# Values, index key and token scalars of a hybrid attention block as one token-major product, 340 columns wide

## The chip, the cores and the metric

The kernel runs on one core of a Trainium2 chip. The metric is the time of one execution on the device in microseconds (us); the median of three runs before the change is 1101.5 us. The engines are TensorE (PE in the profile, with its weight loads as PEld), VectorE (DVE), ScalarE (ACT), GpSimd (POOL) and SyncE (SP). Each works through its own list of instructions in order and waits on semaphores for the others.

## What is computed

Two layers of a block on 256 tokens with 1024 features: a mixer (sparse attention and a gated delta rule from one input projection), cross attention to a memory, and a gated feed-forward. The change touches the start of the mixer alone. Cut to that:

```
h = rms_norm(x) * gain
proj = h @ w_in
a_q, a_k, a_v, i_q, i_k, i_w, b_qkv, b_a, b_b, g_a, g_b = split(proj)
q, k, qi, ki = rope(a_q), rope(a_k), rope(i_q), rope(i_k)      # ki: 64 columns, the index key
g    = -exp(a_log) * softplus(b_a + dt_bias)                    # 8 columns per token
beta = sigmoid(b_b)                                             # 8 columns per token
score = sum over 4 index heads of i_w * relu(qi . ki)           # i_w: 4 columns per token
sel = the 64 best keys of each token, by score
y_a = softmax attention of q over the selected k and v          # v: 256 columns
y_b = gated_delta_rule(conv(b_qkv), g, beta)
```

## The kernel before, in words

Activations lie feature-major: `h` has features on partitions and tokens in columns. A weight is read in **slabs** of 128 x 1024 floats (512 KB), 322 in all, in the order of the list `ORDER` that `stream_of` makes. SyncE fetches each slab into one of five places (`RAWS`), ScalarE rounds it into one of four places (`HIGHS`; function `highs`, L381), GpSimd (a few times VectorE) makes the rest that the rounding lost (function `lows`, L391), and TensorE then multiplies three times: high by high, low by high, high by low (function `product`, L494 to L496). So every logical product is three matmuls. A slab's fetch waits until the slab five before it has been used, its rounding until the one four before it has.

Most products are **feature-major**: the weight block is the stationary operand, 256 tokens stream past, and the result has features on partitions. They take one slab each, 8 blocks of 128 features, 24 matmuls 256 columns wide (`wide_half`). The values are **token-major**: a 128 x 128 piece of `h` is the stationary operand and the weight's columns stream past.

At the start of the mixer TensorE's list is: index queries `iq` (2 slabs), `small` (1 slab: feature-major, 20 token scalars and the 64 index-key columns padded to 128 rows), keys `k` (2 slabs), the transposes of the 20 scalar rows (L613), values `v` (2 slabs, token-major), queries `q0` (2 slabs), the index `logits` (L636, which wait for the rotated index query and key), `q1` to `q3` (2 slabs each), and the `decay` products (L670). Then come `bk0`, `bk1` and so on. PSUM banks are handed out in turn by `claim`, which waits for the last reader of a bank: `bk1` takes the bank of `q2`, and so waits for its rotation.

VectorE's list there: rotation of `iq` (L1879 to L1884), of the index key (L1894 to L1899), of `k`; then the **gate chain** (L1912 to L1926: sixteen columns, thirteen small steps that go to ScalarE and back for an exponential and a logarithm); four products `g_upto` (L1930), `beta` (L1932), the rotation of `q0`, and the score of token tile 0 (L1950 to L1953), followed by its top-64 search.

ScalarE's list decides when slabs are rounded. `copy` first calls `high_parts`, which rounds slabs up to a fixed count, and then waits for what it copies. One place matters: the relus of the second token tile wait for the first tile's score, because they overwrite its input, and no slab behind the second one of `q2` is rounded ahead of them:

```
                    if c == 1:

                        act.wait_ge(*dve_idx.at(layer, ("score", 0)))
```

## Time and profile before

| | |
|---|---|
| median of three runs (lowest, highest) | 1101.5 us (1101.43, 1101.6) |
| profiled execution, first to last instruction (span) | 1099.9 us |
| around the span, median less span | 1.6 us |
| mean granted TensorE clock | 0.999 of full speed |
| TensorE / VectorE / ScalarE / GpSimd busy | 99% / 51% / 51% / 61% |
| HBM read | 179.47 MB |

The profiled execution's own time outside its span is not recorded apart; the difference to the median stands for it. How to read it: matmuls are pipelined, so the busy share of TensorE says that something is always in flight, not that it works at its peak. The distance from one start to the next tells what a matmul costs.

### The profile page before, as it was taken

The page shows a single profiled execution, that of the slowest core. Times are in us where ns is not written, and L with a number is a line of the kernel's source. Part 1 is how long each engine was busy: PE and PEld are TensorE (multiplying, and loading weights), DVE is VectorE, ACT ScalarE, POOL GpSimd, SP SyncE. Part 2 cuts the span into 40 slices and gives each one's busy share as a digit, 9 for nine tenths or more (in the row PEclk, how much of TensorE's full clock was granted, in tenths as well). Part 3 has the DMA queues.
Part 4 walks back from the last instruction along what each step waited for, and adds up shares of the span by engine and source line. Part 5 has one row for each costly group of instructions (what it writes and reads, how often), then busy time and mean ns, then how long its engine had stood idle before and what let it go on. Part 6 is the DMA issues. An engine that isn't in the chain of part 4 may idle for free.

```text
span 1099.9 us, 19903 instructions
## 1 busy us (share of the span) xinstructions
PE 1089.6 (99%) x8135; PEld 1014.0 (92%) x8138; DVE 559.5 (51%) x1082; ACT 561.2 (51%) x888; POOL 670.2 (61%) x351
## 2 busy tenths in 40 slices
PE   8999999999999999999999999999999999999997
PEld 7999999998898999999999999999989979999996
DVE  6788479354515631223358866793644344212234
ACT  7645864435655544444464567544356554444442
POOL 4876769627673457654377758685378454586442
PEclk9999999999999999999999999999999999999999
DMA  7443544624543655555555444445155255555553
GB/s 291 173 154 135 188 130 163 180 74 170 194 153 125 205 188 186 180 189 180 184 173 173 157 141 164 152 156 163 69 194 194 97 181 178 191 179 187 187 180 112
DMA packets 63337, 183.37 MB, mean 167 GB/s; under 512 B 18576, under 2 KB 19088, under 8 KB 63248
## 3 DMA queue, kind: packets, MB, share of 16 engines
q1 hardware_dynamic: 47936, 172.48, 45.3%
q10 hardware_dynamic: 15312, 9.64, 3.4%
q8 instruction: 64, 1.05, 0.4%
q14 instruction: 25, 0.20, 0.1%
HBM read 179.47 MB, written 2.62 MB: 166 GB/s over the span
## 4 chain that ended last, share of the span: by engine, by line
PE 97%; ACT 1%; DVE 1%; DMA 1%; POOL 0%; issue 0%; SPq 0%; DVEq 0%; ACTq 0%; POOLq 0%
PE psum L494 28%; PE psum L495 27%; PE psum L496 27%; PE psum L658 1%; PE psum L985 1%; PE psum L964 1%; PE psum L699 1%; PE psum L1086 1%; PE psum L588 1%; PE psum L879 1%; PE psum L872 1%; PE psum L754 1%; DMA sb_raw<-weights 1%; PE psum L682 1%; PE psum L843 0%; PE psum L670 0%
## 5 line engine op out<-in xcount | busy, mean ns | idle before, releaser
L391 POOL TENSOR_TENSOR sb_low<-sb_raw,sb_high 128x1024 fp32r<-128x1024 f32 x257 | 616.5, 2413 | 337.3 <-ACT sb_high L381 323.1
L381 ACT ACTIVATE sb_high<-sb_raw 128x1024 fp32r<-128x1024 f32 x322 | 340.1, 1061 | 406.4 <-DMA sb_raw<-weights 361.6
L494 PE MATMUL psum<-sb_h_high,sb_high 128*128 128x256 f32 x1640 | 463.9, 283 | 0.0
L495 PE MATMUL psum<-sb_h_low,sb_high 128*128 128x256 f32 x1640 | 463.3, 282 | 0.0
L496 PE MATMUL psum<-sb_h_high,sb_low 128*128 128x256 f32 x1640 | 462.5, 282 | 0.0
L494 PEld LDWEIGHTS psum<-sb_h_high,sb_high 128*128 128x128 f32 x1640 | 310.3, 189 | 1.8 <-DVE sb_region_c L1879 0.3
L496 PEld LDWEIGHTS psum<-sb_h_high,sb_low 128*128 128x128 f32 x1640 | 308.6, 188 | 0.0
L495 PEld LDWEIGHTS psum<-sb_h_low,sb_high 128*128 128x128 f32 x1640 | 307.7, 188 | 0.9
L391 DVE TENSOR_TENSOR sb_low<-sb_raw,sb_high 128x1024 fp32r<-128x1024 f32 x65 | 85.4, 1314 | 95.4 <-ACT sb_high L381 95.0
L1992 DVE SCALAR_TENSOR_TENSOR sb_conv<-psum,sb_param,sb_conv 128x255 f32<-128x255 f32 (+1 forms) x144 | 58.2, 473 | 37.0 <-ACT sb_conv L1405 36.8
L2248 DVE SCALAR_TENSOR_TENSOR sb_sq<-sb_th,psum 128x512 f32<-128x512 f32 x22 | 15.1, 687 | 110.0 <-ACT sb_th L1610 110.0
L495 PE MATMUL psum<-sb_low,sb_ff 128*128 128x512 f32 x176 | 69.7, 396 | 0.0
L496 PE MATMUL psum<-sb_high,sb_ff 128*128 128x512 f32 x176 | 69.7, 396 | 0.0
L494 PE MATMUL psum<-sb_high,sb_ff 128*128 128x512 f32 x176 | 69.7, 396 | 0.0
L496 PEld LDWEIGHTS psum<-sb_high,sb_ff 128*128 128x128 f32 x176 | 33.1, 188 | 8.0
L495 PEld LDWEIGHTS psum<-sb_low,sb_ff 128*128 128x128 f32 x176 | 33.2, 188 | 7.2
L494 PEld LDWEIGHTS psum<-sb_high,sb_ff 128*128 128x128 f32 x176 | 33.1, 188 | 7.2
L494 PE MATMUL psum<-sb_mem_high,sb_high 128*128 128x256 f32 x128 | 38.2, 298 | 1.0 <-DVE sb_mem_low L1734 1.0
L2252 DVE SCALAR_TENSOR_TENSOR psum<-sb_sq,psum 128x512 f32<-128x512 f32 x21 | 14.6, 696 | 48.1 <-PE psum L496 48.1
L496 PE MATMUL psum<-sb_mem_high,sb_low 128*128 128x256 f32 x128 | 36.1, 282 | 0.0
L495 PE MATMUL psum<-sb_mem_low,sb_high 128*128 128x256 f32 x128 | 36.0, 282 | 0.0
L2207 DVE TENSOR_REDUCE sb_tiny<-psum 128x2 f32<-128x512 f32 x8 | 5.6, 694 | 50.4 <-PE psum L964 50.4
(307 smaller groups left out, 1549.0 us busy)
## 6 DMA issues: line engine op xcount, KB each, us to landing
sb_raw<-weights SPq DMA_DIRECT2D x322, 512.0 KB, 3.2
sb_pre_gain<-pre_gains ACTq DMA_DIRECT2D x6, 512.0 KB, 4.4
sb_post_gain<-post_gains ACTq DMA_DIRECT2D x6, 512.0 KB, 4.5
sb_kx<-mem SPq DMA_DIRECT2D x2, 512.0 KB, 4.4
sb_x<-x SPq DMA_DIRECT2D x1, 1024.0 KB, 10.7
t_dram<-sb_sq ACTq DMA_DIRECT2D x4, 256.0 KB, 2.9
out<-sb_x SPq DMA_DIRECT2D x4, 256.0 KB, 2.0
m_dram<-sb_m ACTq DMA_DIRECT2D x8, 64.0 KB, 2.1
```

The lines of the kernel that those rows point to most:

```text
L381: nc.scalar.activation(high[:, n % HIGHS, :], raw[:, n % RAWS, :], ACT.Copy).then_inc(high_ready, 1)
L391: eng.tensor_tensor(low[:, k, :], raw[:, k, :], high[:, n % HIGHS, :].bitcast(F32), ALU.subtract).then_inc(low_ready[k], 1)
L494: pe.matmul(out, a[0], b[0], start=start, stop=False, **kw)
L495: pe.matmul(out, a[0], b[1], start=False, stop=False, **kw)
L496: return pe.matmul(out, a[1], b[0], start=False, stop=stop, **kw)
L588: tr = pe.transpose(o[:, k * P:(k + 1) * P], xn[:, c, b * P:(b + 1) * P], ident)
L658: mm = pe.matmul(o[:, i * P:(i + 1) * P], conv[:, hd, c * P:(c + 1) * P], conv[:, other + hd, c * P:(c + 1) * P], start=True, stop=True)
L682: mm = pe.matmul(misc[:, 16 * c + 2 * j + b:16 * c + 2 * j + b + 1], sq[:, j % 2, b * S + c * P:b * S + (c + 1) * P], one, start=True, sto ...
L699: pe.matmul(o[:, i * keys:(i + 1) * keys], q[:, hd, c * P:(c + 1) * P], kT[:, hd // (HEADS // KV_HEADS), 0:keys], start=True, stop=False, ...
L1992: V.scalar_tensor_tensor(out=conv[:, blk, d:S], in0=bank(CONV_SLOTS[j])[:, b * S:(b + 1) * S - d], scalar=tap(3 - d, blk), in1=conv[:, blk ...
L2248: link(V.scalar_tensor_tensor(out=sq[:, i % 2, :], in0=th[:, i % 2, :], scalar=1.0, in1=bank(("gate", i)), op0=ALU.add, op1=ALU.mult), dve ...
L2252: V.scalar_tensor_tensor(out=ff_tok if turned else bank(("up", i)), in0=sq[:, i % 2, :], scalar=0.5, in1=bank(("up", i)), op0=ALU.mult, op ...
```

## The change

The values, the index key and the token scalars become one weight of 256 + 64 + 20 = 340 columns (`BY_TOKEN`), laid into three slabs of 3, 3 and 2 feature blocks (`KS_OF`). TensorE multiplies it token-major: two token tiles, each in a bank of its own (5 and 6), eight feature blocks, three matmuls, that is 48 matmuls 340 columns wide in the place of the 24 of `small` and the 48 of `v`, all 256 wide. The number of slabs stays 322. The scalars come out token-major and aren't transposed any more; the index key is, after `k`. VectorE now does the gate chain ahead of the rotations of `k` and of the index key. ScalarE copies the index key, the scalars and, behind the logarithm, the values.

```diff
@@ -50,6 +50,9 @@
 HALF = KT * P
 FF_SLOTS = FF // 256
 TOKENWISE = IDX_HEADS + 2 * G_HEADS
+KV_COLS = KV_HEADS * DH
+BY_TOKEN = KV_COLS + IDX_DIM + TOKENWISE
+KS_OF = tuple(range(3 * b, min(3 * b + 3, KT)) for b in range(3))
 both = lambda part, *which: [(part, i, b) for i in which for b in range(2)]
 
 
@@ -57,7 +60,7 @@
     first, more = layer == 0, layer + 1 < DEPTH
     return (
         (both("xk", 0, 1) + [("xk", 2, 0)] if first else both("xk", 1, 2))
-        + both("iq", 0) + [("small", 0, 0)] + both("k", 0) + both("v", 0) + both("q", *range(4))
+        + both("iq", 0) + [("vs", 0, b) for b in range(3)] + both("k", 0) + both("q", *range(4))
         + both("bk", *range(4)) + both("bq", *range(4)) + both("bv", *range(4)) + both("ga", *range(4)) + both("gb", *range(4))
         + ([("xk", 2, 1)] if first else []) + both("xk", 3) + both("xv", 0) + [("xv", 1, 0)]
         + both("out", *range(4))
@@ -230,7 +233,7 @@
         idx_val = ra_t[:, 1024:1536].rearrange("p (c s) -> p c s", c=TILES)
         iq = rb_t[:, 0:512].rearrange("p (b t) -> p b t", b=2)
         ik = rb_t[:, 512:768]
-        small_feat = rb_t[0:TOKENWISE, 768:1024]
+        ik_tok = rb_t[:, 768:768 + 2 * IDX_DIM].rearrange("p (c n) -> p c n", c=TILES)
         rope_tmp = rc_t[:, 0:1024].rearrange("p (b n) -> p b n", b=2)
         p1 = ra_t[:, :].rearrange("p (h s) -> p h s", h=HEADS)
         t_up = grp(ra_t)
@@ -604,24 +607,20 @@
                 pe.wait_ge(*dve_part.at(layer, ("h_low", "mix", 1, 0)))
 
                 wide(("iq", 0), h, (dve_rope, "iq"), (4,), waits={4: dve_part.at(layer, ("h_low", "mix", 1, 1))})
-                o = claim(("small", 0), (dve_rope, "ik"), (5,))
-                wide_half(o[:, 0:S], HALF_AT[layer, "small", 0, 0], h).then_inc(slots.sem, mark(slots, ("small", 0)))
+                by_token = [claim(("vs", c), (act_copy, "v"), (5 + c,)) for c in range(TILES)]
+                for b in range(3):
+                    w = weights_here(HALF_AT[layer, "vs", 0, b])
+                    for c in range(TILES):
+                        for k in KS_OF[b]:
+                            at = slice((k - KS_OF[b][0]) * BY_TOKEN, (k - KS_OF[b][0] + 1) * BY_TOKEN)
+                            mm = product(by_token[c][:, 0:BY_TOKEN], pick(h, lambda t: t[:, k, c * P:(c + 1) * P]), pick(w, lambda t: t[:, at]), k == 0, k == KT - 1)
+                    mm.then_inc(slots.sem, mark(slots, ("vs", 0) if b == 2 else ("vs", 0, b)))
                 wide(("k", 0), h, (dve_rope, "k"))
-                o = claim("small_tok", (dve_gate, "x"), (3,), False)
-                pe.wait_ge(*act_copy.at(layer, "small"))
+                o = claim("ik_turned", (dve_rope, "ik"), (3,), False)
+                pe.wait_ge(*act_copy.at(layer, "ik"))
                 for c in range(TILES):
-                    tr = pe.transpose(o[:, c * TOKENWISE:(c + 1) * TOKENWISE], small_feat[:, c * P:(c + 1) * P], ident[0:TOKENWISE, 0:TOKENWISE])
-                tr.then_inc(pe_t.sem, mark(pe_t, "small_tok"))
-                o = claim(("v", 0), (act_copy, "v"))
-                for b in range(2):
-                    w = weights_here(HALF_AT[layer, "v", 0, b])
-                    for c in range(TILES):
-                        for k4 in range(4):
-                            k = 4 * b + k4
-                            mm = product(o[:, c * 256:(c + 1) * 256], pick(h, lambda t: t[:, k, c * P:(c + 1) * P]),
-                                         pick(w, lambda t: t[:, k4 * 256:(k4 + 1) * 256]), k == 0 and c == 0, k == KT - 1 and c == 1,
-                                         skip_group_check=True)
-                    mm.then_inc(slots.sem, mark(slots, ("v", 0) if b else ("v", "first")))
+                    tr = pe.transpose(o[0:IDX_DIM, c * P:(c + 1) * P], ik_tok[:, c, :], ident)
+                tr.then_inc(pe_t.sem, mark(pe_t, "ik_turned"))
                 wide(("q", 0), h, (dve_rope, ("q", 0)))
 
                 pe.wait_ge(*dve_rope.at(layer, "iq"))
@@ -1360,11 +1359,10 @@
                     act.wait_ge(masks_loaded, 32)
                     nc.scalar.activation(after_t[:, :], after, ACT.Copy).then_inc(after_ready, 1)
 
-                high_parts(ahead(("small", 0), 3))
-
-                copy(small_feat, bank(("small", 0))[0:TOKENWISE, 0:S], slots, ("small", 0), act_copy, "small")
-                copy(small, bank("small_tok")[:, 0:2 * TOKENWISE].rearrange("p (c n) -> p c n", c=TILES), pe_t, "small_tok", act_copy, "small_tok")
-                act.wait_ge(*act_copy.at(layer, "small_tok"))
+                by_token = psum[:, 5:7, :]
+                copy(ik_tok, by_token[:, :, KV_COLS:KV_COLS + IDX_DIM], slots, ("vs", 0), act_copy, "ik")
+                nc.scalar.activation(small, by_token[:, :, KV_COLS + IDX_DIM:BY_TOKEN], ACT.Copy).then_inc(act_copy.sem, act_copy.mark("small"))
+                act.wait_ge(*act_copy.at(layer, "small"))
                 nc.scalar.activation(beta, small[:, :, 12:20], ACT.Tanh, scale=0.5).then_inc(act_gdn.sem, act_gdn.mark("beta"))
                 nc.scalar.activation(a_exp, param_t[:, R_ALOG:R_ALOG + 8], ACT.Exp).then_inc(act_gdn.sem, act_gdn.mark("a"))
                 act.wait_ge(*dve_gate.at(layer, "abs"))
@@ -1372,7 +1370,7 @@
                 act.wait_ge(*dve_gate.at(layer, "w"))
                 nc.scalar.activation(ga_ln, ga_w, ACT.Ln).then_inc(act_gdn.sem, act_gdn.mark("ln"))
 
-                copy(flat(v_tok), bank(("v", 0)), slots, ("v", 0), act_copy, "v", scale=0.5)
+                nc.scalar.activation(v_tok, by_token[:, :, 0:KV_COLS], ACT.Copy, scale=0.5).then_inc(act_copy.sem, act_copy.mark("v"))
 
                 for c in range(TILES):
                     keys = (c + 1) * P
@@ -1885,16 +1883,16 @@
 
                 def rotate_ik():
 
-                    src = bank(("small", 0))[64:P, 0:S]
-                    tmp = rope_tmp[64:P, 1, 0:S]
-                    low_parts(ahead(("small", 0), 2))
-                    dve.wait_ge(*act_copy.at(layer, "small"))
-                    for lo in (64, 96):
+                    src = bank("ik_turned")[0:IDX_DIM, 0:S]
+                    tmp = rope_tmp[0:IDX_DIM, 1, 0:S]
+                    low_parts(ahead("ik_turned", 2))
+                    dve.wait_ge(*pe_t.at(layer, "ik_turned"))
+                    for lo in (0, 32):
                         o = lo ^ 32
-                        V.tensor_tensor(rope_tmp[lo:lo + 32, 1, 0:S], bank(("small", 0))[o:o + 32, 0:S], rope[o:o + 32, 3, :], ALU.mult)\
+                        V.tensor_tensor(rope_tmp[lo:lo + 32, 1, 0:S], src[o:o + 32], rope[o:o + 32, 3, :], ALU.mult)\
                             .then_inc(dve_rope.sem, dve_rope.mark(("partner", "ik", lo)))
-                    dve.wait_ge(*dve_rope.at(layer, ("partner", "ik", 96)))
-                    link(V.tensor_tensor(src, src, rope[64:P, 2, :], ALU.mult), dve_rope, ("cos", "ik"))
+                    dve.wait_ge(*dve_rope.at(layer, ("partner", "ik", 32)))
+                    link(V.tensor_tensor(src, src, rope[0:IDX_DIM, 2, :], ALU.mult), dve_rope, ("cos", "ik"))
                     V.tensor_tensor(ik[64:P], src, tmp, ALU.add).then_inc(dve_rope.sem, dve_rope.mark("ik_upper"))
                     link(V.tensor_tensor(ik[0:64], src, tmp, ALU.add), dve_rope, "ik")
 
@@ -1904,12 +1902,10 @@
                     dve.wait_ge(masks_loaded, 32)
                     dve.wait_ge(tables_act, 1)
                 rotate("iq", ("iq", 0), iq, 2, 2, 32, "iq", 0)
-                rotate_ik()
-                rotate("k", ("k", 0), kT, 2, 0, 64, "k", 0)
 
                 link(V.tensor_copy(upto_psum, upto), dve_gate, "upto")
-                dve.wait_ge(*act_copy.at(layer, "small_tok"))
-                link(V.tensor_tensor(ga_x, bank("small_tok")[:, 0:2 * TOKENWISE].rearrange("p (c n) -> p c n", c=TILES)[:, :, 4:12], heads(param_t[:, R_DT:R_DT + 8], TILES), ALU.add), dve_gate, "x")
+                dve.wait_ge(*act_copy.at(layer, "small"))
+                link(V.tensor_tensor(ga_x, small[:, :, 4:12], heads(param_t[:, R_DT:R_DT + 8], TILES), ALU.add), dve_gate, "x")
                 link(V.tensor_scalar(ga_abs, ga_x, -1.0, None, ALU.mult), dve_gate, "minus")
                 link(V.tensor_tensor(ga_abs, ga_x, ga_abs, ALU.max), dve_gate, "abs")
                 dve.wait_ge(*act_gdn.at(layer, "e"))
@@ -1924,6 +1920,8 @@
                 V.tensor_copy(g_tok, ga_x).then_inc(dve_gate.sem, dve_gate.mark("g"))
                 link(V.tensor_copy(g_round, ga_x), dve_gate, "g_round")
                 link(V.tensor_tensor(g_rest, ga_x, g_round.bitcast(F32), ALU.subtract), dve_gate, "g_rest")
+                rotate("k", ("k", 0), kT, 2, 0, 64, "k", 0)
+                rotate_ik()
                 for c in range(TILES):
 
                     for part, g_part in enumerate((g_round.bitcast(F32), g_rest)):
@@ -2318,11 +2316,9 @@
                 continue
             name = "xk" if name == "nk" else name
             to = stream[n]
-            if name == "small":
-                piece = blocks(np.concatenate([tokenwise, np.zeros((D, 64 - TOKENWISE), np.float32), part("ik")], 1))
-                to.reshape(P, KT, P)[:, :, 0:piece.shape[2]] = piece
-            elif name == "v":
-                to[:] = blocks(part("v")[512 * b:512 * (b + 1)]).reshape(P, HALF)
+            if name == "vs":
+                piece = blocks(np.concatenate([part("v"), part("ik"), tokenwise], 1))[:, list(KS_OF[b])]
+                to[:, 0:len(KS_OF[b]) * BY_TOKEN] = piece.reshape(P, -1)
             elif name in ("gate", "up") and i == 0 and layer + 1 == DEPTH:
                 to[:] = blocks(mats[name][512 * b:512 * (b + 1), 0:256]).reshape(P, HALF)
             elif name == "down":
```

VectorE at the start of the mixer in layer 0, before: from the end of the `iq` rotation (out `sb_region_b`) to the first step of the gate chain (`128x16`).

```order
L1884 TENSOR_TENSOR sb_region_b<-psum,sb_region_c 128x512
L1894 TENSOR_TENSOR sb_region_c<-psum,sb_rope_tables 32x256 x2
L1897 TENSOR_TENSOR psum<-psum,sb_rope_tables 64x256
L1898 TENSOR_TENSOR sb_region_b<-psum,sb_region_c 64x256
L1899 TENSOR_TENSOR sb_region_b<-psum,sb_region_c 64x256
L1879 TENSOR_TENSOR sb_region_c<-psum,sb_rope_tables 64x512 x2
L1883 TENSOR_TENSOR psum<-psum,sb_rope_tables 128x512
L1884 TENSOR_TENSOR sb_k_rope<-psum,sb_region_c 128x512
L1910 COPY psum<-sb_const 128x128
L1912 TENSOR_TENSOR psum<-psum,sb_param 128x16
```

The same engine and place now, from the `iq` rotation on:

```order
L1882 TENSOR_TENSOR sb_region_b<-psum,sb_region_c 128x512
L1906 COPY psum<-sb_const 128x128
L1908 TENSOR_TENSOR psum<-sb_tiny,sb_param 128x16
L1909 TENSOR_SCALAR sb_tiny<-psum 128x16
L1910 TENSOR_TENSOR sb_tiny<-psum,sb_tiny 128x16
```

And the end of the gate chain now, up to the first `g_upto` product (out `sb_g_high`):

```order
L1922 TENSOR_TENSOR sb_tiny<-psum,sb_g_round 128x16
L1877 TENSOR_TENSOR sb_region_c<-psum,sb_rope_tables 64x512 x2
L1881 TENSOR_TENSOR psum<-psum,sb_rope_tables 128x512
L1882 TENSOR_TENSOR sb_k_rope<-psum,sb_region_c 128x512
L1892 TENSOR_TENSOR sb_region_c<-psum,sb_rope_tables 32x256 x2
L1895 TENSOR_TENSOR psum<-psum,sb_rope_tables 64x256
L1896 TENSOR_TENSOR sb_region_b<-psum,sb_region_c 64x256
L1897 TENSOR_TENSOR sb_region_b<-psum,sb_region_c 64x256
L1928 TENSOR_TENSOR sb_g_high<-psum,sb_g_round 128x1024
```

Both rotations moved from ahead of the gate chain to behind it, the index key's last; the instructions are the same in number and size.

ScalarE in layer 0, before: roundings (L381), the copy of the feature-major scalars (`20x256`), the copy of the transposed ones (`128x40`), the gate chain's functions, roundings, values.

```order
L381 ACTIVATE sb_high<-sb_raw 128x1024 x3
L1327 ACTIVATE sb_region_b<-psum 20x256
L381 ACTIVATE sb_high<-sb_raw 128x1024 x2
L1327 ACTIVATE sb_tiny<-psum 128x40
L1368 ACT_TABLE_LOAD
L1368 ACTIVATE sb_tiny<-sb_tiny 128x16
L1369 ACTIVATE sb_tiny<-sb_param 128x8
L1371 ACTIVATE psum<-sb_tiny 128x16
L1373 ACT_TABLE_LOAD
L1373 ACTIVATE sb_tiny<-sb_tiny 128x16
L381 ACTIVATE sb_high<-sb_raw 128x1024 x2
L1327 ACTIVATE sb_v<-psum 128x512
```

The same place now, with the index key copied as `128x128`:

```order
L384 ACTIVATE sb_high<-sb_raw 128x1024 x5
L1326 ACTIVATE sb_region_b<-psum 128x128
L1364 ACTIVATE sb_tiny<-psum 128x40
L1366 ACT_TABLE_LOAD
L1366 ACTIVATE sb_tiny<-sb_tiny 128x16
L1367 ACTIVATE sb_tiny<-sb_param 128x8
L1369 ACTIVATE psum<-sb_tiny 128x16
L1371 ACT_TABLE_LOAD
L1371 ACTIVATE sb_tiny<-sb_tiny 128x16
L1373 ACTIVATE sb_v<-psum 128x512
```

All five roundings now stand ahead of the first copy, and the values are copied ahead of the next two roundings.

## Rows read from the trace of the kernel before

**Rows 1.** The page's line of busy us, shares of the span and counts.

```profile
PE 1089.6 (99%) x8135; PEld 1014.0 (92%) x8138; DVE 559.5 (51%) x1082; ACT 561.2 (51%) x888; POOL 670.2 (61%) x351
```

**Rows 2.** The waits of TensorE: who for whom, us in total, times, longest.

```profile
PE psum L452 <- DVE sb_th L1723: 1.5, 1, 1.5
```

**Rows 3.** Timeline of TensorE, layer 0: start us, us, engine, line, operation, out<-in.

```profile
33.38 0.28 PE L494 MATMUL psum<-sb_h_high,sb_high 128*128 128x256 f32 x1
...
53.99 1.68 PE L636 MATMUL psum<-sb_region_b 64*128 64x128 f32 x16
...
73.03 0.58 PE L670 MATMUL psum<-sb_g_high,sb_after 128*128 128x512 f32 x1
...
250.98 0.39 PE L494 MATMUL psum<-sb_high,sb_mem_high 128*128 128x512 f32 x1
...
253.54 0.40 PE L496 MATMUL psum<-sb_high,sb_mem_low 128*128 128x512 f32 x1
```

**Rows 4.** Timeline of VectorE, layer 0; in brackets the idle time before and who ended it.

```profile
38.27 0.88 DVE L1894 TENSOR_TENSOR sb_region_c<-psum,sb_rope_tables 32x256 f32<-32x256 f32 x2 [0.28 <-ACT sb_region_b L1327]
...
40.12 0.43 DVE L1899 TENSOR_TENSOR sb_region_b<-psum,sb_region_c 64x256 f32<-64x256 f32 x1
42.29 1.41 DVE L1879 TENSOR_TENSOR sb_region_c<-psum,sb_rope_tables 64x512 f32<-64x512 f32 x2 [1.75 <-PE psum L496]
...
45.20 0.30 DVE L1910 COPY psum<-sb_const 128x128 f32<-128x128 f32 x1
...
49.12 1.22 DVE L1930 TENSOR_TENSOR sb_g_high<-psum,sb_g_round 128x1024 fp32r<-128x1024 f32 x1
...
53.66 2.38 DVE L1932 TENSOR_SCALAR sb_tiny<-sb_tiny 128x16 f32<-128x16 f32 x1
...
59.16 0.35 DVE L1950 TENSOR_SCALAR psum<-sb_region_a,sb_tiny 128x128 f32<-128x128 f32 x1
```

**Rows 5.** Timeline of ScalarE, layer 0.

```profile
42.60 1.06 ACT L381 ACTIVATE sb_high<-sb_raw 128x1024 fp32r<-128x1024 f32 x1 [1.37 <-DMA sb_raw<-weights]
43.56 0.18 ACT L1327 ACTIVATE sb_tiny<-psum 128x40 f32<-128x40 f32 x1
...
46.16 0.19 ACT L1371 ACTIVATE psum<-sb_tiny 128x16 f32<-128x16 f32 x1 [0.79 <-DVE sb_tiny L1914]
```

**Rows 6.** Timeline of GpSimd, layer 0.

```profile
41.30 4.84 POOL L391 TENSOR_TENSOR sb_low<-sb_raw,sb_high 128x1024 fp32r<-128x1024 f32 x2 [0.19 <-ACT sb_high L381]
...
48.91 9.44 POOL L391 TENSOR_TENSOR sb_low<-sb_raw,sb_high 128x1024 fp32r<-128x1024 f32 x4 [2.76 <-ACT sb_high L381]
63.15 14.18 POOL L391 TENSOR_TENSOR sb_low<-sb_raw,sb_high 128x1024 fp32r<-128x1024 f32 x6 [4.80 <-ACT sb_high L381]
```

**Rows 7.** VectorE's L1734 in its two forms, and GpSimd beside it.

```profile
10.54 3.23 DVE L1734 SCALAR_TENSOR_TENSOR sb_mem_low<-psum,sb_param,sb_mem_high 128x256 fp32r<-128x256 f32 x8 [0.34 <-ACT sb_mem_high L1202]
...
342.95 5.68 DVE L1734 SCALAR_TENSOR_TENSOR sb_mem_low<-sb_mem_feat,sb_param,sb_mem_high 128x256 fp32r<-128x256 f32 x4 [1.45 <-ACT sb_mem_high L1193]
...
10.29 2.38 POOL L391 TENSOR_TENSOR sb_low<-sb_raw,sb_high 128x1024 fp32r<-128x1024 f32 x1 [2.00 <-DVE sb_low L391]
...
345.87 2.47 POOL L391 TENSOR_TENSOR sb_low<-sb_raw,sb_high 128x1024 fp32r<-128x1024 f32 x1 [0.86 <-ACT sb_high L381]
```

**Rows 8.** Layer 1: timelines of ScalarE, VectorE, GpSimd and TensorE.

```profile
585.62 1.06 ACT L381 ACTIVATE sb_high<-sb_raw 128x1024 fp32r<-128x1024 f32 x1 [1.81 <-DMA sb_raw<-weights]
...
589.20 0.19 ACT L1371 ACTIVATE psum<-sb_tiny 128x16 f32<-128x16 f32 x1 [2.08 <-DVE sb_tiny L1914]
...
596.69 0.16 DVE L1932 TENSOR_SCALAR sb_tiny<-sb_tiny 128x16 f32<-128x16 f32 x1
...
586.76 2.40 POOL L391 TENSOR_TENSOR sb_low<-sb_raw,sb_high 128x1024 fp32r<-128x1024 f32 x1 [0.49 <-ACT sb_high L381]
...
604.04 7.27 POOL L391 TENSOR_TENSOR sb_low<-sb_raw,sb_high 128x1024 fp32r<-128x1024 f32 x3 [2.48 <-ACT sb_high L381]
...
616.06 0.58 PE L670 MATMUL psum<-sb_g_high,sb_after 128*128 128x512 f32 x1
```

## The prediction, written before the changed kernel ran

> **What bounds the kernel now.** I read the page first: TensorE is busy 99% of the span, everyone else at most 61% [rows 1]. A busy share alone can mislead for pipelined matmuls, so the list of waits came second: TensorE's longest wait is 1.5 us, at the very start [rows 2], and none lies in the stretch that the change touches, in either layer. So TensorE's own stream is the bound there, and taking columns off it pays, as long as no wait appears that had been covered. Third came TensorE's timeline, for what a matmul costs: the distance between starts, not the 0.28 us shown. From the first matmul of `small` at 33.38 to the logits at 53.99 are 20.61 us; seven slabs are 168 matmuls, 256 wide, and the two scalar transposes with their changes of kind take the rest; 168 x 0.120 = 20.16. At 512 columns eleven steps from 250.98 to 253.54 give 0.233 us [rows 3]. Last, the timelines of VectorE, ScalarE and GpSimd in the same stretch, to see how much cover their chains have: that is where this case is decided.
>
> **TensorE's part.** Per layer 24 + 48 matmuls of 256 columns go (72 x 0.120 = 8.64 us) and 48 of 340 come. No row has 340 columns. The bounds are 0.120 (as 256 wide) and 0.233 (as 512 wide) [rows 3]; cost grows with width, so I take the straight line between them, 0.120 + 84/256 x 0.113 = 0.157 us, nearer the 256 end. 48 x 0.157 = 7.54 us, a saving of 1.1 us per layer, 2.2 in all. The two transposes stay two, moved behind `k`; I cost the move at nothing. The slabs, their bytes and the rounding work are the same in number, and a slab is used in 18, 18 and 12 matmuls instead of 24, which asks for the next ones sooner.
>
> The Trainium skill ("TensorE: Matmul & The Clock Gate", Back-to-back issue gap) gives N/2.4 GHz + 2.5 ns. By that rule, as an estimate, 340 columns cost 0.144 us and the saving is 1.7 us per layer; the trace differs from it, 0.120 against its 0.109 at 256 columns. By it the sum below would be about 1 us lower.
>
> **VectorE's chain, layer 0.** Before, the index key is rotated from 38.27 to 40.55 and `k` from 42.29 to 45.20 [rows 4], while the scalars are still on their way. Now both rotations (2.3 + 2.9 = 5.2 us) stand behind the gate chain, and the logits wait for the index key. So the question is when the gate chain can start and end.
>
> Its input comes through ScalarE, which now rounds five slabs before it copies. The last of them (the second of `q0`) is fetched when the second new slab has been used, at 33.38 + 36 x 0.157 = 39.04. Before, the fetch waited for the slab that ended at 39.15 and the rounding started at 42.60 [rows 5]; now 42.5. Before, the scalars' copy followed at 43.56; now one more short copy stands between (estimate 0.3, from the 0.18 of the small one): the scalars are ready at about 43.95.
>
> The first gate step changes its operands. It was `psum<-psum,sb_param`; now it is `psum<-sb_tiny,sb_param`, with both inputs in SBUF. What that means is in two rows of one line, L1734: with one input in PSUM eight instructions take 3.23 us while GpSimd's 2.38 us operation runs beside them; with both in SBUF four take 5.68 us instead of 1.6, and the last ends at 348.63, 0.28 after GpSimd's operation from 345.87 to 348.34 [rows 7]. An instruction with both inputs in SBUF does not get through beside a GpSimd operation; it waits for its end. `beta` (L1932), all in SBUF, shows the same: 2.38 us from 53.66, where GpSimd's operations run, and 0.16 at 596.69, in a gap between two [rows 4, 6, 8]. The Trainium skill says so too ("SBUF — State Buffer", Who interferes with whom): two SBUF inputs contend with a GpSimd instruction that reads SBUF, and the one that comes second is blocked until the first has finished.
>
> GpSimd works on the two `q0` slabs from 41.30 to 46.14 [rows 6], now 0.1 us earlier at most. The first gate step therefore starts at 43.95 and ends at 46.15, not at 44.15. Its bounds are 0.18 (no conflict) and 2.4 (a whole operation). From there to the exponential (46.16 before) it is 0.45 us: 46.6, that is 0.4 later than before. The rest of the chain takes as long as before, to 49.12 + 0.4; then come the rotations, 5.2 us: the index key is ready at 54.8. Before, the logits started at 53.99. So TensorE, which could have been there at 52.9, starts them 0.8 us late: the saving is gone in that wait.
>
> Everything behind is shifted more: `g_upto` starts at 54.8 instead of 49.12, 5.65 later. `beta` gives some of it back: GpSimd's four operations, from 48.91 to 58.35 before, run some 0.9 later now (0.4 for the chain, 0.5 for the values' copy put ahead of the roundings) and end at about 59.3, just when `beta` comes; nothing follows them until the score is done. `beta` costs 0.2 instead of 2.38. The score of tile 0 then starts 3.5 us later than at 59.16.
>
> That score releases the relus of tile 1, and behind them the rounding of the first `q3` slab, whose rest GpSimd makes from 63.15 on, after 4.80 us of idling [rows 6]. TensorE reaches that slab 48 matmuls before 73.03, at 67.2 [rows 3]: a cover of 67.2 - 65.5 = 1.7 us. Now the rest is ready at 63.15 + 3.5 + 2.4 = 69.05, and TensorE, 0.8 late, arrives at 68.0. It goes on at 69.1: **+1.9 us in layer 0**. Queued behind the waiting relus are all of ScalarE's roundings, so this is the wait that counts; from the next slab on GpSimd (2.4 us) is faster than TensorE (2.88 us) again.
>
> **Layer 1.** The rounding that was at 585.62 is at 585.5 [rows 8], the scalars are ready at 587.0, and GpSimd is in the operation that began at 586.76 (now 586.65, to 589.05). The first gate step ends at 589.1, the exponential is at 589.55, 0.35 later. The logits start 0.7 late by the same count. `beta` was short before, so nothing is given back: the score is 0.35 + 5.2 = 5.6 us later. GpSimd's operation of 604.04 moves to 609.65 and ends at 612.05. TensorE was there at 616.06 - 5.8 = 610.25, now at 610.95; it goes on at 612.1: **+1.85 us**.
>
> **Sum.** +1.9 + 1.85 = +3.8 us on a span of 1099.9: 1103.7. The median is 1.6 above that span, so the forecast is 1105.3 us. No term is owed for the 2.2 us of saved columns: in both layers the end is set by VectorE's chain. Only the columns of the first two new slabs count, since they set when the last rounding is released: the chain moves with 36 of them. Priced as 256 wide (36 x 0.037 = 1.3 us earlier in each layer) the sum is +1.2, 1102.7; priced as 512 wide (36 x 0.076 = 2.7 later) it is +9.2, 1110.7.
>
> **Rivals.**
>
> *No conflict at the first gate step.* For: it is 16 columns wide and might slip in between GpSimd's accesses, and no row shows so small an operation with two tensors in SBUF. Against: L1932 is as small and did wait. Then the exponential waits for ScalarE's table load alone: 0.6 earlier than before in layer 0 (it had idled 0.79, the scalars come 0.2 later), 1.55 earlier in layer 1 (it had idled 2.08). Layer 0: logits 0.25 early, `beta` held until the four operations end, score 2.4 later, slab ready at 67.95: +0.75. Layer 1: logits 1.1 early, score 3.8 later, slab at 610.2: 0. Together +0.8: 1102.3 us.
>
> *The saved columns come through.* The chain is covered everywhere and 2.2 us go: 1099.3 us. For it speaks that TensorE waits nowhere now. Against: the covers are 1.7 us at the `q3` slab in layer 0 and about 3.8 in layer 1, and 5.2 us of rotations are put in front of what has them. It needs the gate chain to end some 3 us sooner than before.
>
> *`beta` held as well: clearly slower.* In both layers `beta` comes within 0.1 us of the end of GpSimd's run. If it comes just after the last operation has begun, because a rounding was late, it is held for up to 2.4 us, and the score, the `q3` slab and TensorE with it. The point is whether the last of the four operations ends before VectorE has done `g_upto`. In one layer that makes +2.1: 1107.4 us.
>
> *340 columns cost like 512*: 1110.7 us, as above.
>
> **How the numbers follow.** The forecast 0.62, no conflict 0.17, `beta` held 0.10, dear columns 0.05, saving comes through 0.06. A measurement of this kernel can tell about 0.2% from no change, 2.2 us. Slower by more than that (over 1103.7) are nearly all of the forecast's outcomes (0.57), `beta` held and dear columns: 0.72. Within it are the case without conflict, a few of the forecast's, and half of the last: 0.24. Faster: 0.04. The range reaches from the case without conflict with some room, 1101.8, to the one with `beta` held, 1107.5; outside are the saving that comes through, dear columns and little else.
>
> **What the changed profile would show.** Matmuls with 340 columns start 0.157 us apart. L1908 of the changed kernel (the first gate step) takes about 2.2 us in both layers and ends with a GpSimd operation; at 0.18 us the first rival is right. The gate chain then starts 0.4 us later than before, and `beta` (L1930 there) is short in layer 0. TensorE has waits that it had not: for `dve_rope` ahead of the logits, 1.9 us in layer 0 and 1.8 in layer 1, and for the rest of the first `q3` slab, 1.1 us in each. If the second of these is missing, the forecast is wrong, wherever the time comes out.

## The result, and the profile after

The changed kernel takes 1106.32 us (median of four runs, 1106.18 to 1107.84), the kernel before 1101.51: a ratio of 1.0044, 95% interval 1.0032 to 1.0057. So the change made it 0.4% slower. A repetition (e11 below) gave 1.0049 (1.0036 to 1.0062). The forecast was 1105.3 us, slower. The profiled execution has a span of 1104.5 us, 4.6 more than before. What follows first shows where these 4.6 us are, and then, by twelve runs, what causes them.

First the list of TensorE's waits in the changed kernel (who waits for whom: us in total, times, longest). Against [rows 2] two are new, the first and the last shown: the index logits (L635) wait for VectorE's rotation of the index key, and a product (L497) waits for GpSimd to finish the rest of a slab. Both stand in the stretch that the change touches.

```profile
PE psum L635 <- DVE sb_region_b L1897: 4.4, 2, 2.5
PE psum L455 <- DVE sb_th L1721: 1.5, 1, 1.5
PE psum L497 <- DVE sb_mem_low L1732: 1.0, 1, 1.0
PE psum L461 <- DVE sb_kx L1727: 1.0, 2, 0.7
PE psum L497 <- POOL sb_low L394: 0.9, 1, 0.9
```

Then TensorE's timeline (start us, us, engine, line, operation; in brackets the idle time before and who ended it), which answers to [rows 3]. From the first 340 wide matmul to the last are 47 steps, 7.33 us: 0.156 us each, where 0.157 was forecast.

```profile
33.75 0.32 PE L497 MATMUL psum<-sb_high,sb_h_high 128*128 128x340 f32 x1
...
41.08 0.32 PE L499 MATMUL psum<-sb_high,sb_h_low 128*128 128x340 f32 x1
...
55.60 1.68 PE L635 MATMUL psum<-sb_region_b 64*128 64x128 f32 x16 [2.48 <-DVE sb_region_b L1897]
...
76.08 0.58 PE L669 MATMUL psum<-sb_g_high,sb_after 128*128 128x512 f32 x1
...
600.38 1.65 PE L635 MATMUL psum<-sb_region_b 64*128 64x128 f32 x16 [1.91 <-DVE sb_region_b L1897]
...
614.66 0.36 PE L497 MATMUL psum<-sb_h_high,sb_high 128*128 128x256 f32 x1 [0.92 <-POOL sb_low L394]
```

Layer 1 shows both waits, as forecast. Layer 0 has no wait for a slab, and the prediction said of that wait that without it the forecast is wrong, wherever the time comes out. And yet from the logits (55.60) to the decay products (76.08) it needs 20.48 us where before it needed 19.04. The busy time by stretch says why (from:to, length, PE busy us and count, granted clock, DMA share, GB/s):

```profile
53.00:56.00 3.00, 0.52 (x8) 1.00 0.53 183
56.00:57.00 1.00, 1.00 (x14) 1.00 0.00 0
57.00:58.00 1.00, 1.00 (x6) 0.55 0.00 0
58.00:60.00 2.00, 2.00 (x12) 0.50 0.00 0
60.00:61.00 1.00, 1.00 (x8) 0.74 0.00 0
61.00:62.00 1.00, 1.00 (x10) 1.00 0.00 0
```

Behind the idle stretch (53.1 to 55.6) the granted clock is 0.50, 1.2 GHz, for some 3 us; the 256 wide matmuls there start 0.213 us apart and not 0.120. That makes this part 1.45 us longer. The Trainium skill describes it ("TensorE: Matmul & The Clock Gate", What's actually happening): a monitor halves the clock of a TensorE that has been idle. The trace agrees, and e5 and e10 below put it to the test.

VectorE's timeline answers to [rows 4], ScalarE's to [rows 5], GpSimd's to [rows 6]:

```profile
44.83 2.15 DVE L1908 TENSOR_TENSOR psum<-sb_tiny,sb_param 128x16 f32<-128x16 f32 x1 [6.14 <-ACT sb_tiny L1364]
...
50.38 1.41 DVE L1877 TENSOR_TENSOR sb_region_c<-psum,sb_rope_tables 64x512 f32<-64x512 f32 x2
...
55.54 1.23 DVE L1928 TENSOR_TENSOR sb_g_high<-psum,sb_g_round 128x1024 fp32r<-128x1024 f32 x1
...
60.07 0.17 DVE L1930 TENSOR_SCALAR sb_tiny<-sb_tiny 128x16 f32<-128x16 f32 x1
...
63.36 0.35 DVE L1948 TENSOR_SCALAR psum<-sb_region_a,sb_tiny 128x128 f32<-128x128 f32 x1
```

```profile
43.40 1.06 ACT L384 ACTIVATE sb_high<-sb_raw 128x1024 fp32r<-128x1024 f32 x1 [2.36 <-DMA sb_raw<-weights]
44.37 0.26 ACT L1326 ACTIVATE sb_region_b<-psum 128x128 f32<-128x128 f32 x1
44.52 0.20 ACT L1364 ACTIVATE sb_tiny<-psum 128x40 f32<-128x40 f32 x1
...
47.43 0.19 ACT L1369 ACTIVATE psum<-sb_tiny 128x16 f32<-128x16 f32 x1 [1.08 <-DVE sb_tiny L1910]
```

```profile
44.54 2.40 POOL L394 TENSOR_TENSOR sb_low<-sb_raw,sb_high 128x1024 fp32r<-128x1024 f32 x1 [0.91 <-ACT sb_high L384]
50.66 9.36 POOL L394 TENSOR_TENSOR sb_low<-sb_raw,sb_high 128x1024 fp32r<-128x1024 f32 x4 [3.72 <-ACT sb_high L384]
67.36 4.75 POOL L394 TENSOR_TENSOR sb_low<-sb_raw,sb_high 128x1024 fp32r<-128x1024 f32 x2 [7.35 <-ACT sb_high L384]
```

These rows show three things. VectorE idles 6.14 us ahead of the first gate step, where it used to rotate. That step (L1908) takes 2.15 us and ends within 0.05 us of GpSimd's operation beside it (44.54 + 2.40). And from the gate chain (44.83) to the score (63.36) VectorE has one unbroken row of work, 18.5 us long, in which it waits for another engine only twice, for ScalarE's two functions, 0.96 us together. The row simply starts too late.

**Where the 4.6 us are.** I measure one stretch of TensorE's list in each layer, from the first index-query matmul to the first of `bk0` (27.90 to 79.17 in layer 0 after the change). Before it is 48.49 us in each layer; after, 51.27 and 50.28. Layer 0: -1.31 (from the first matmul of the product to the point where the logits could start are 19.30 us, not 20.61), +2.55 of standing still ahead of the logits, +1.45 of low clock, +0.09 in the index query: +2.78. Layer 1: -1.31, +1.98 ahead of the logits, +1.12 for the slab: +1.79. Together 4.57 of the 4.6.

### The profile page after: what moved, and what is told of

The parts are those of the page before. It is cut to its first block, busy times and chain, and to the rows that moved or that the text cites. A ratio compares the mean times of both kernels' runs of the same rounds, so it can differ in the third digit from the quotient of the medians.

```text
span 1104.5 us, 19808 instructions
## 1 busy us (share of the span) xinstructions
PE 1088.7 (99%) x8090; PEld 1013.1 (92%) x8090; DVE 565.2 (51%) x1082; ACT 559.9 (51%) x888; POOL 672.1 (61%) x351
## 4 chain that ended last, share of the span: by engine, by line
PE 93%; DVE 3%; DMA 1%; ACT 1%; issue 1%; POOL 0%; SPq 0%; DVEq 0%; ACTq 0%; POOLq 0%
PE psum L497 26%; PE psum L498 26%; PE psum L499 26%; PE psum L657 1%; PE psum L984 1%; DMA sb_raw<-weights 1%; PE psum L963 1%; PE psum L698 1%; PE psum L1085 1%; PE psum L591 1%; PE psum L878 1%; PE psum L871 1%; PE psum L753 1%; PE psum L681 1%; ACT sb_high L384 1%
## 5 line engine op out<-in xcount | busy, mean ns | idle before, releaser
L497 PE MATMUL psum<-sb_h_high,sb_high 128*128 128x256 f32 x1624 | 461.4, 284 | 0.9 <-POOL sb_low L394 0.9
L498 PE MATMUL psum<-sb_h_low,sb_high 128*128 128x256 f32 x1624 | 458.5, 282 | 0.0
L497 PEld LDWEIGHTS psum<-sb_h_high,sb_high 128*128 128x128 f32 x1624 | 307.1, 189 | 3.3 <-issue 1.8
L497 PE MATMUL psum<-sb_high,sb_ff 128*128 128x512 f32 x176 | 69.7, 396 | 0.0
L497 PEld LDWEIGHTS psum<-sb_high,sb_ff 128*128 128x128 f32 x176 | 33.1, 188 | 7.2
L497 PE MATMUL psum<-sb_mem_high,sb_high 128*128 128x256 f32 x128 | 38.2, 298 | 1.0 <-DVE sb_mem_low L1732 1.0
```

Source lines behind the costliest of these rows:

```text
L497: pe.matmul(out, a[0], b[0], start=start, stop=False, **kw)
L498: pe.matmul(out, a[0], b[1], start=False, stop=False, **kw)
```

## The experiments

For each kernel its two stretches in us, in one profiled execution (before: 48.49 and 48.49), and its median beside that of the kernel before, run next to it on the same chip. The ratio is worked out from all runs, so it can differ a little from that of the two medians:

| kernel | layer 0 | layer 1 | median | before | ratio, 95% |
|---|---|---|---|---|---|
| changed | 51.27 | 50.28 | 1106.32 | 1101.51 | 1.0044 (1.0032 to 1.0057) |
| e1 gate step from PSUM | 49.90 | 48.33 | 1103.88 | 1102.30 | 1.0016 (1.0007 to 1.0024) |
| e2 index key first | 53.75 | 51.80 | 1109.71 | 1102.30 | 1.0064 (1.0051 to 1.0077) |
| e3 score first | 52.86 | 52.52 | 1110.70 | 1102.30 | 1.0082 (1.0059 to 1.0106) |
| e4 both | 53.81 | 53.28 | 1115.66 | 1102.30 | 1.0119 (1.0106 to 1.0132) |
| e5 long filler | 52.20 | 51.74 | 1109.77 | 1102.64 | 1.0063 (1.0049 to 1.0077) |
| e6 before, new order | 49.25 | 49.00 | 1104.33 | 1102.64 | 1.0016 (1.0007 to 1.0025) |
| e7 changed, old order | 54.24 | 53.08 | 1112.88 | 1102.64 | 1.0093 (1.0079 to 1.0107) |
| e8 copy sooner | 51.22 | 49.63 | 1107.89 | 1102.64 | 1.0048 (1.0034 to 1.0062) |
| e9 as e8, and beta later | 47.88 | 47.75 | 1101.49 | 1101.91 | 0.9994 (0.9985 to 1.0002) |
| e10 short filler | 51.39 | 50.34 | 1107.05 | 1101.91 | 1.0048 (1.0034 to 1.0062) |
| e11 changed again | 51.57 | 50.69 | 1107.60 | 1101.91 | 1.0049 (1.0036 to 1.0062) |
| e12 as e9, and score 1 sooner | 48.26 | 47.48 | 1101.59 | 1102.05 | 0.9995 (0.9986 to 1.0004) |

**e1: is it the two SBUF inputs?**

```diff
-link(V.tensor_tensor(ga_x, small[:, :, 4:12], ...), dve_gate, "x")
+link(V.tensor_tensor(ga_x, psum[:, 5:7, KV_COLS + IDX_DIM + 4:KV_COLS + IDX_DIM + 12], ...), dve_gate, "x")
```

> The changed kernel with one operand changed: the first gate step reads the scalars from the product's PSUM banks and not from ScalarE's copy in SBUF; it still waits for that copy, so its place and its wait are the same. Theory (two SBUF inputs are blocked by the GpSimd operation beside them): the step takes 0.18 us and not 2.15. In layer 0 ScalarE is busy until 46.35, so the exponential comes only 1.0 us sooner; in layer 1 2.0 sooner. Logits wait 1.4 us in layer 0, too short for the clock to fall, and none in layer 1; the wait for the first q3 slab's rest is about 0.9 in each. Sum about -3.5: 1102.8 us. Rival (the step waits for something else, such as ScalarE's copy or a semaphore): it still takes about 2.15 us and the time stays at 1106.3.

The step's row on VectorE, and GpSimd's beside it:

```profile
44.71 0.18 DVE L1908 TENSOR_TENSOR psum<-psum,sb_param 128x16 f32<-128x16 f32 x1 [6.35 <-ACT sb_tiny L1364]
```

```profile
44.43 2.39 POOL L394 TENSOR_TENSOR sb_low<-sb_raw,sb_high 128x1024 fp32r<-128x1024 f32 x1 [0.91 <-ACT sb_high L384]
```

Same place, same wait, same neighbour: 0.18 us instead of 2.15, in layer 1 as well. The cause of that term is shown: it is the second input from SBUF beside a GpSimd operation. The time falls to 1.0016 of the kernel before, 1.58 us over it where 1.3 was expected; waits of 1.5 us (index key, layer 0) and 0.9 (slab, in each layer) are left, and the clock stays at 1.00.

**e2, e3, e4: are TensorE's waits in series?** e2 swaps two calls. e3 moves six instructions, the four `g_upto` products, `beta` and its neighbour, behind the score of tile 0. e4 does both.

```diff
-rotate("k", ("k", 0), kT, 2, 0, 64, "k", 0)
 rotate_ik()
+rotate("k", ("k", 0), kT, 2, 0, 64, "k", 0)
```

> The changed kernel with one edit: VectorE rotates the index key ahead of k. The logits can then start when TensorE arrives (index key ready at 52.6 in layer 0, TensorE there at 53.1), but k, g_upto, beta, the rotation of q0 and the score come at the same time as now. Theory (both waits hang on one chain, in series): nothing is won, TensorE idles about 3.4 us in layer 0 and 2.8 in layer 1 for the rest of the first q3 slab instead, and if the clock falls after such a wait it costs up to 1.4 us in each: 1105.9 to 1108.7, I expect 1107.3. Rival (waits add up, each can be taken away alone): the 4.4 us of waiting for the index key and 1.4 of low clock go: 1100.5.

The wait of the logits goes, and waits of 3.77 and 2.92 us for the slab come, each with the low clock (some 25 and 15 slow matmuls). TensorE's timeline, then its stretches; in layer 0 the clock fell at 69.3, while TensorE was still waiting:

```profile
70.50 0.55 PE L497 MATMUL psum<-sb_h_high,sb_high 128*128 128x256 f32 x1 [3.77 <-POOL sb_low L394]
```

```profile
70.00:72.00 2.00, 1.50 (x7) 0.50 0.00 0
72.00:74.00 2.00, 2.00 (x11) 0.50 0.03 8
74.00:76.00 2.00, 2.00 (x12) 0.50 0.00 0
76.00:78.00 2.00, 2.00 (x18) 0.96 0.51 125
```

One long wait is dearer than the two short ones: e2 is 7.4 us slower than the kernel before beside it, the changed kernel 4.8. TensorE stands still for 6.7 us in all and not 5.3, and has the low clock in both layers.

```diff
-for c in range(TILES):
-    for part, g_part in enumerate((g_round.bitcast(F32), g_rest)):
-        V.tensor_tensor(g_upto[part][:, c, :, :], ...)
-link(V.tensor_scalar(beta, beta, 0.5, 0.5, ALU.mult, ALU.add), dve_gate, "beta")
-V.tensor_scalar(half_gdn, ...)
 rotate("q0", ("q", 0), q[:, 0:2, :], 2, 0, 64, ("q", 0), 1)
 ...
     link(V.scalar_tensor_tensor(out=val if hd == 3 else acc, ...), dve_idx, ("score", c) ...)
+if c == 0:
+    ...
```

> The changed kernel with one edit: the four g_upto products, beta and its neighbour stand behind the score of token tile 0 and not ahead of it (4.9 us of VectorE's work moved). The relus of tile 1 and ScalarE's roundings are released 4.9 us sooner; the wait of the logits stays 2.5 and 1.9 us and so does the low clock. Theory: in layer 0 TensorE already comes later than the slab's rest, so nothing changes there; in layer 1 the 0.9 us wait goes: 1105.4 us. Rival (the score's chain is what costs the time in both layers, as the prediction had it for layer 0): -1.9 or more, 1104.4 or lower.

> Both edits of the two runs before together (index key ahead of k, g_upto and beta behind the score of tile 0). Theory of two waits in series: now both covers hold, the 4.4 us of waiting for the index key, the 0.9 for the slab and the 1.4 of low clock all go: 1099.5 us, which is the kernel before less the saved 2.2 us of columns. Rival (each edit gives what it gives alone, they add up): 1106.4. Rival two (the saving of columns does not come through to the end even with all waits gone, because later waits take it): about 1101.5, as the kernel before.

Both of my expectations fell, by 5 and 16 us. In e3 the logits wait as before (2.75 and 2.03 us) and the slab no longer does, but in layer 1 a decay product waits 3.10 us. Its six runs lie between 1107.67 and 1116.51 us, wider than those of any other kernel here; that spread isn't explained, so only e3's being slower is safe, not its size. What I had not seen is a third wait behind the two. The waits of e4, then the end of the score of tile 1 on VectorE and the start of the fourth decay product on TensorE:

```profile
PE psum L667 <- DVE sb_region_a L1944: 7.6, 2, 3.8
PE psum L667 <- DVE sb_sel_bias L1977: 2.9, 2, 1.8
```

```profile
79.22 0.48 DVE L1944 SCALAR_TENSOR_TENSOR sb_region_a<-sb_region_a,sb_tiny,psum 128x256 f32<-128x256 f32 x1
```

```profile
79.76 0.39 PE L667 MATMUL psum<-sb_const_b 128*128 128x512 bf16 x1 [3.77 <-DVE sb_region_a L1944]
```

Banks are handed out in turn, and two of the four decay products get banks whose last reader is the end of tile 0's top-64 search (`sel_bias`) and the score of tile 1. Moving six instructions behind the score of tile 0 doesn't take them off VectorE's way to these two. It brought the first release sooner and made the others later: the search ends at 74.38 and the score of tile 1 at 79.70, and in the changed kernel at 72.31 and 77.63 (`beta`, now beside GpSimd, took 2.38 us again). So the series has three links, one chain of VectorE feeds them all, and a new order inside that chain only chooses which of them TensorE meets.

**e5, e10: does the idle stretch lower the clock, and what does that hide?** Extra matmuls in layer 0, ahead of the wait for the index key: 22 in e5, 10 in e10.

```diff
 pe.wait_ge(*dve_rope.at(layer, "iq"))
+if layer == 0:
+    ...
+    for _ in range(22):
+        pe.matmul(psum[:, first, 0:P], iq[0:64, 0, 0:P], iq[0:64, 0, 0:P], start=True, stop=True)
 pe.wait_ge(*dve_rope.at(layer, "ik"))
```

> The changed kernel with 22 extra small matmuls (64 rows by 128 columns, results overwritten) in layer 0 ahead of the wait for the rotated index key, about 2.2 us of TensorE work in the 2.5 us that it idles there. Nothing else is moved. Theory (after the idle stretch the granted clock is 0.5 for some 3 us, which costs 1.4 us; it falls because TensorE idled): the 14 slow matmuls behind the logits are gone, TensorE is 1.4 us sooner at the first q3 slab and waits 0.9 us for its rest there, as in layer 1: 1105.8 us, 0.5 less. Rival (the clock falls for another reason): the slow matmuls stay and the time too, 1106.3.

No slow matmul is left in layer 0, but the filler ran for 5.0 us and not 2.2 (the trace has 44 instructions for the 22, 0.114 us apart), so the time says nothing. With a shorter one:

> The changed kernel with 10 extra matmuls (two passes each, 20 x 0.114 = 2.3 us) in layer 0 ahead of the wait for the rotated index key; in e5 the 22 took 5.0 us and so hid what was asked. Theory (the clock falls because TensorE idles there, and the low clock hides the wait for the first q3 slab): no slow matmuls behind the logits, logits start as in the changed kernel, and TensorE waits 0.9 us for the first q3 slab in layer 0 too: 0.5 us less than the changed kernel, 1.0040 of the kernel before. Rival (low clock and slab wait are independent costs, or the slab wait is not there): 1.4 us less, 1.0031.

```profile
53.60 2.50 PE L632 MATMUL psum<-sb_region_b 64*128 64x128 f32 x20
56.55 0.71 PE L641 MATMUL psum<-sb_region_b 64*128 64x128 f32 x7 [0.45 <-DVE sb_region_b L1903]
```

```profile
70.89 0.36 PE L497 MATMUL psum<-sb_h_high,sb_high 128*128 128x256 f32 x1 [0.95 <-POOL sb_low L394]
```

With TensorE at work the clock stays at 1.00, and the slab wait that the prediction had for layer 0 appears, 0.95 us. By the profiles both claims hold: two traces with a filler in layer 0 have no low clock there, the two without (the changed kernel and e11) have it. The stretch of layer 0 is only 0.18 us shorter than in e11, for most of what the low clock cost now goes to the slab. The time moved by 0.55 us against e11, as expected, but the two intervals overlap almost wholly, so the size isn't shown by the times. (e11, the changed kernel again, was expected with waits of 2.5, 1.9 and 0.9 us; it had 2.69 and 1.94, the low clock in both layers, and no wait for a slab.)

**e6, e7: product or order?** e6 is the kernel before with the two rotations behind the gate chain; e7 the changed kernel with them ahead of it.

```diff
 rotate("iq", ("iq", 0), iq, 2, 2, 32, "iq", 0)
-rotate_ik()
-rotate("k", ("k", 0), kT, 2, 0, 64, "k", 0)
 ...
 link(V.tensor_tensor(g_rest, ga_x, g_round.bitcast(F32), ALU.subtract), dve_gate, "g_rest")
+rotate("k", ("k", 0), kT, 2, 0, 64, "k", 0)
+rotate_ik()
```

> The kernel before (two products, scalars transposed) with VectorE's order alone changed: gate chain first, then the rotations of k and the index key. Theory (the order costs only together with the product, which has k, the scalars and the index key ready later): the chain starts 0.8 us sooner in layer 0, the index key is ready at 53.5, so the logits don't wait; g_upto is 4.4 us later, the score 2.3 later in layer 0 (beta short) and 3.3 in layer 1; TensorE waits 0.6 us for the first q3 slab in layer 0 and not in layer 1: 0.6 us over the kernel before, 1102.1 by its median. Rival (the order alone is what costs): +4 or more, 1105.5.

The same in the other direction, in the changed kernel:

> The changed kernel with VectorE's old order: k and the index key are rotated ahead of the gate chain. Theory (the product makes k ready at 47.0 only, so the gate chain would start at 52.5 and ScalarE, which waits in it with all its roundings queued behind, would round the first q1 slab 5 us too late): slower than the changed kernel, TensorE idles about 5 us ahead of q1 in each layer, partly in place of the waits it has now: about 1113 us. Rival (the new order is the cause of the loss): with the old order the saved columns come through, 1099.3 to 1102.

e6: 1.0016, in the stretches +0.76 and +0.51; the logits don't wait, the slab is waited for 0.53 and 0.25 us. The order alone costs little, 1.7 us by the medians, if more than the 0.6 I had. e7: 1112.88, forecast 1113, and that it hit is partly luck: I had 5 us of idling ahead of `q1` in each layer, and it has 2.35, 1.01 for a bank, and the low clock. (It rotates `k` ahead of the index key, the kernel before the other way round; the index key is ready last now.) The product with the rotations ahead costs 10.2 us, with the new order 4.8. So the product is what costs, and the new order makes it cheaper: the product delivers `k`, the scalars and the index key within 3 us of each other, so 5.2 us of rotations have nowhere to hide.

**e8, e9, e12: start the chain sooner.** VectorE's 6.14 us of idling end with ScalarE's copy, which stands behind a fifth rounding that waits for its slab.

```diff
-copy(ik_tok, ..., slots, ("vs", 0), act_copy, "ik")
+copy(ik_tok, ..., slots, ("vs", 0), act_copy, "ik", 2)
```

> The changed kernel with one number changed: ScalarE rounds four slabs and not five ahead of the copies of the index key and the scalars (the fifth, the second of q0, comes behind the values' copy). The scalars are then ready at about 41.7 in layer 0, and the exponential starts some 3.3 us sooner, even with the first gate step still blocked by GpSimd until 43.6. Theory (VectorE's chain from the scalars to the scores sets every one of TensorE's waits): the logits don't wait, the clock stays up, the first q3 slab's wait is 0.3 us or less, the decay's banks are free in time: -5.5 us, 1100.8, between 1100.3 and 1102.3. Rival (one of the waits has another cause, or the second q0 slab, rounded late, takes the gain): 1104 or more.

The chain started 2.9 us sooner against the product, the logits no longer wait, and the time did not move: 1107.89, 1.0048 of the kernel before beside it. (The first gate step is still held, for 1.60 us.) VectorE's and GpSimd's timelines of layer 0, and TensorE's:

```profile
57.61 2.09 DVE L1930 TENSOR_SCALAR sb_tiny<-sb_tiny 128x16 f32<-128x16 f32 x1
59.73 0.15 DVE L1931 TENSOR_SCALAR sb_tiny<-sb_param 128x1 f32<-128x1 f32 x1
```

```profile
47.85 11.81 POOL L394 TENSOR_TENSOR sb_low<-sb_raw,sb_high 128x1024 fp32r<-128x1024 f32 x5 [3.71 <-ACT sb_high L384]
66.83 4.71 POOL L394 TENSOR_TENSOR sb_low<-sb_raw,sb_high 128x1024 fp32r<-128x1024 f32 x2 [7.16 <-ACT sb_high L384]
```

```profile
69.33 0.36 PE L497 MATMUL psum<-sb_h_high,sb_high 128*128 128x256 f32 x1 [2.23 <-POOL sb_low L394]
```

`beta` now comes while GpSimd is in the last of its five operations and is held to its end (59.66), 2.09 us. It is the prediction's rival with `beta` held, met in another kernel. The slab is late by 2.23 us in each layer, and in layer 0 the clock falls behind that.

```diff
-link(V.tensor_scalar(beta, beta, 0.5, 0.5, ALU.mult, ALU.add), dve_gate, "beta")
-V.tensor_scalar(half_gdn, ...)
 rotate("q0", ("q", 0), q[:, 0:2, :], 2, 0, 64, ("q", 0), 1)
 ...
     link(V.scalar_tensor_tensor(out=val if hd == 3 else acc, ...), dve_idx, ("score", c) ...)
+if c == 0:
+    link(V.tensor_scalar(beta, beta, 0.5, 0.5, ALU.mult, ALU.add), dve_gate, "beta")
+    V.tensor_scalar(half_gdn, ...)
```

> The kernel of e8 with one more edit: beta and its neighbour stand behind the score of token tile 0, where GpSimd idles, and not ahead of it. In e8 beta was blocked by GpSimd for 2.1 us in each layer and the rest of the first q3 slab came 2.2 us late. Theory (that block is what ate e8's gain): beta takes 0.2 us, the score comes 2.3 us sooner, TensorE meets the first q3 slab ready in both layers, the bank of the fourth decay product is free just in time, the clock never falls: the kernel before less its 2.2 us of columns, up to 0.4 us of small waits left: 0.9980 to 0.9984 of the kernel before, 1099.7 us where that takes 1101.5. Rival (a further wait, on the bank that the score of tile 1 gives back or on ScalarE, takes its place): no faster than the kernel before.

All long waits are gone: the stretches take 47.88 and 47.75 us, 0.6 and 0.7 less than before the change, and the median is 6.1 us under that of e11 beside it. Against the kernel before it is 0.9994, not the 0.9980 to 0.9984 expected. The 1.31 us of each layer are there (53.95 - 34.65 = 19.30), but 0.6 of them go again: logits to `bk0` takes 22.7 us and not 22.12. Half of that is the third link (the fourth decay product starts 0.3 us late, just behind the score of tile 1, which ends at 75.55):

```profile
75.60 0.39 PE L667 MATMUL psum<-sb_const_b 128*128 128x512 bf16 x1
```

The other half stands at the first `q3` slab, whose rest is ready at 67.26: its first matmul starts at 67.40, 0.34 us behind the one before it where 0.12 is usual, and the next 0.20 behind that; layer 1 shows the same.

```profile
67.06 0.28 PE L499 MATMUL psum<-sb_h_high,sb_low 128*128 128x256 f32 x1
67.40 0.36 PE L497 MATMUL psum<-sb_h_high,sb_high 128*128 128x256 f32 x1
```

```diff
 if c == 1:
     low_parts(ahead(("logits", 0, 1), 5))
-    rotate_q(1)
 ...
     link(V.scalar_tensor_tensor(out=val if hd == 3 else acc, ...), dve_idx, ("score", c) ...)
 ...
+if c == 1:
+    rotate_q(1)
```

> The kernel of e9 with one more edit: VectorE scores token tile 1 ahead of the rotation of q1, not behind it. In e9 the stretch from the logits to bk0 takes 22.7 us where the kernel before takes 22.1, and the fourth decay product starts 0.5 us late: its bank is given back by the score of tile 1. Theory (that bank is the one wait left in the stretch): the fourth decay product doesn't wait, q1's rotation still ends 0.5 us ahead of bk0, which takes its bank, and the stretch from the first index-query matmul to bk0 is 47.2 us in each layer instead of 47.8 (48.5 before the change): 0.6 us less in each layer, 0.9982 of the kernel before, 0.9994 for e9. Rival (bk0 now waits for the rotation of q1, or the rotations of q2 and q3 come late for bk1 and bk2): no faster than e9.

The fourth decay product no longer waits, and the rival has its share: `bk1`, which lies behind the stretch, now waits 0.4 us for a rotation in each layer. The loss at the `q3` slab stays (logits to `bk0` takes 22.4 us).

```profile
82.58 0.39 PE L497 MATMUL psum<-sb_h_high,sb_high 128*128 128x256 f32 x1 [0.38 <-DVE sb_gates L1882]
```

Layer 1's stretch is 1.0 us under that of before, layer 0's only 0.2 (it has a 0.5 us wait for a slab's rest in `q0`, ahead of the logits); 0.9995. By its time neither version, e9 or e12, can be told from the kernel before.

## Why the prediction came out as it did

- **340 columns at 0.157 us:** 0.156. The estimate of 0.144 by the rule of the Trainium skill ("TensorE: Matmul & The Clock Gate", Back-to-back issue gap) is below what the chip did here. The stretch gave 1.31 us per layer, not 1.1. The rest is in the transposes, whose move the prediction cost at nothing: from the last matmul ahead of them to the second behind them it was 0.66 us with the 20 scalar rows (41.90 to 42.56), and is 0.46 with the index key (46.87 to 47.33).
- **First gate step blocked, 2.2 us in both layers:** 2.15 and 2.15, and e1 shows the cause. The rule of the Trainium skill ("SBUF — State Buffer", Who interferes with whom) holds for an operation as small as 16 columns.
- **Scalars ready at 43.95:** 44.72. Of the 0.8, 0.37 is that the whole stretch began later; the rest is the slab itself, which landed later than by my count (ScalarE idled 2.36 us for it). In layer 1 the step is on time: 10.50 us behind the product's start, forecast 10.6.
- **`beta` short in both layers:** 0.17 in both. That was luck: in layer 0 GpSimd's run ends at 60.02 and `beta` starts at 60.07, in layer 1 at 604.81 and 604.84. e8 shows the other side of that edge.
- **Waits: 1.9 + 1.1 in layer 0, 1.8 + 1.1 in layer 1.** Layer 1 measured 1.98 and 1.12, +1.79 where +1.85 was forecast. In layer 0 the logits waited 2.55 and the slab was not waited for at all, and there a step failed: the prediction put the clock at nothing. Behind the idle stretch 1.45 us were added at 1.2 GHz, and they took the place of the slab wait (e10): its rest was ready at 69.76 (67.36 + 2.40, the first of the two operations), and TensorE came only at 70.28. By the prediction's own sign the forecast for layer 0 is wrong.
- **How near the number came:** +2.78 instead of +1.9 in layer 0 is the whole difference between the two spans, 1103.7 forecast and 1104.5 measured. It came so near because the two costs stand in for each other. In layer 1 `bk0` starts 9.10 us after the `q3` slab's rest is ready (614.52 to 623.62); by that, as an estimate, layer 0 would have reached it at 78.86 with the clock up, and reached it at 79.17. So the low clock's net cost was some 0.3 us. The rest is mostly that VectorE's chain was later than forecast: from the first index-query matmul to the slab's rest are 41.86 us, forecast 41.43.
- **The rival without a conflict, 1102.3:** its condition is met in e1, 1.58 us over the kernel before, where the rival said 0.8.
- **What the prediction lacked without paying for it:** the third link, the banks of the decay products. Before the change the score of tile 1 ended 1.65 us ahead of the fourth decay product (73.42 against 75.07); with VectorE 4.2 us later that cover was gone too. TensorE was late enough by its other waits to miss it. "The saving comes through" was therefore even less likely than its 0.06.
